# HGRN states, MoBA scores and softmax between the tiles of the projections, HGRN outputs made token by token

## The reference, cut to what matters

```python
hq, hf, hi, hg, mq, mk, mv = jnp.split(h @ w_in, IN_SPLITS, axis=-1)
# HGRN2, per head, chunks of C = 32 tokens
f = lb + (1 - lb) * sigmoid(hf);  k = 1 - f;  b = cumsum(log(f)) within a chunk
q_t = q * exp(b);  k_t = k * exp(-b);  k_end = k * exp(b_last - b)
A = where(causal, q_t @ k_t.T, 0)
o_n = A @ v + q_t @ state            # per chunk n
state = exp(b_last) * state + k_end.T @ v
o = o * rsqrt(mean(o * o, over the 128 of a head) + EPS) * norm_g * silu(hg)
# MoBA: rotary on 32 of 128 features of mq and mk, then
p = softmax(where(causal, mq @ mk.T / sqrt(128), -inf));  o_moba = p @ mv
x = x + concatenate([o_hgrn, o_moba]) @ w_out
```

## Time and profile before

| | before |
|---|---|
| median of 3 runs (lowest, highest) | 862.06 us (860.3, 863.2) |
| the profiled execution: time, span of the core | 863.93 us, 862.1 us |
| granted TensorE clock, mean over the span | 0.963 |
| PE busy | 815.8 us (95%) |
| DVE busy | 565.1 us (66%) |
| ACT busy | 391.2 us (45%) |
| POOL busy | 71.5 us (8%) |
| mean transfer rate over the span | 148 GB/s |

### The profile page before, as it was taken

The page is one execution under the profiler, slowest core; times in us unless marked ns, Lnnn a source line. Parts: engine busy times, 40 slices in busy tenths (PEclk is TensorE's granted clock), DMA queues, the critical chain, the costliest instruction groups (busy, mean ns, idle before and its releaser), DMA issues.

```text
span 862.1 us, 17113 instructions
## 1 busy us (share of the span) xinstructions
PE 815.8 (95%) x7466; PEld 688.3 (80%) x7466; DVE 565.1 (66%) x881; ACT 391.2 (45%) x613; POOL 71.5 (8%) x98
## 2 busy tenths in 40 slices
PE   4999978988999999999999999999998999999996
PEld 3798866777767788888886868597886888888885
DVE  2769975645166889999856777567457566674443
ACT  3546351120053376666754764116256356653333
POOL 1123011202000211111000100000200200000000
PEclk9999996998799999999999999979999999999999
DMA  9772230203004745555586256100482516555201
GB/s 329 290 294 98 98 110 2 101 2 102 1 1 156 272 158 196 195 196 197 195 299 240 98 210 227 52 2 0 177 313 99 194 67 227 196 196 209 86 2 49
DMA packets 66491, 127.93 MB, mean 148 GB/s; under 512 B 3696, under 2 KB 27504, under 8 KB 66288
## 3 DMA queue, kind: packets, MB, share of 16 engines
q1 hardware_dynamic: 65104, 122.92, 39.6%
q0 software_dynamic: 592, 2.69, 0.9%
q10 hardware_dynamic: 720, 1.23, 0.4%
HBM read 125.78 MB, written 1.05 MB: 147 GB/s over the span
## 4 chain that ended last, share of the span: by engine, by line
PE 74%; DVE 15%; ACT 6%; issue 2%; DMA 2%; POOL 0%; DVEq 0%; SPq 0%; ACTq 0%
PE bank L493 21%; PE bank L601 18%; DVE arena L481 7%; PE bank L598 6%; PE bank L699 6%; DVE arena L1865 3%; PE bank L1162 3%; PE bank L1953 3%; DMA ring<-in_w_in_dram 2%; ACT arena L472 2%; PE bank L1414 1%; PE bank L1181 1%; PE bank L2335 1%; PE bank L2077 1%; PE bank L2092 1%
## 5 line engine op out<-in xcount | busy, mean ns | idle before, releaser
L481 DVE SCALAR_TENSOR_TENSOR arena<-ring,arena 128x1024 f16<-128x1024 f32 x194 | 229.5, 1230 | 75.7 <-ACT arena L472 75.3
L493 PE MATMUL bank<-hg,arena 128*128 128x256 f16 x2496 | 275.1, 273 | 1.0 <-DVE arena L481 1.0
L493 PEld LDWEIGHTS bank<-hg,arena 128*128 128x128 f16 x2496 | 243.2, 98 | 32.4 <-issue 2.5
L472 ACT ACTIVATE arena<-ring 128x1024 f16<-128x1024 f32 x194 | 191.9, 1045 | 83.5 <-PE bank L601 51.8
L601 PE MATMUL bank<-arena 128*128 128x256 f16 x1296 | 142.2, 273 | 0.2 <-DVE arena L481 0.2
L601 PEld LDWEIGHTS bank<-arena 128*128 128x128 f16 x1296 | 126.6, 98 | 15.5 <-issue 0.9
L598 PE MATMUL bank<-mix,ring 128*128 128x256 f32 x256 | 55.7, 379 | 1.1 <-ACT arena L1797 1.1
L699 PE MATMUL bank<-hg,ring 128*128 128x256 f32 x224 | 51.5, 391 | 4.7 <-DMA ring<-in_w_in_dram 4.7
L598 PEld LDWEIGHTS bank<-mix,ring 128*128 128x128 f32 x256 | 48.5, 190 | 8.4 <-issue 1.9
L699 PEld LDWEIGHTS bank<-hg,ring 128*128 128x128 f32 x224 | 43.7, 197 | 11.4 <-DMA ring<-in_w_in_dram 5.1
L508 ACT ACTIVATE hg<-h,params 128x256 f16<-128x256 f32 (+1 forms) x48 | 23.9, 499 | 56.4 <-DVE h L2281 42.8
(11 more groups left out here) (365 smaller groups left out, 964.7 us busy)
## 6 DMA issues: line engine op xcount, KB each, us to landing
ring<-in_w_in_dram SPq DMA_DIRECT2D x13, 2048.0 KB, 8.7
ring<-in_ffn_w_up_dram SPq DMA_DIRECT2D x22, 1024.0 KB, 7.4
ring<-in_w_ff_dram SPq DMA_DIRECT2D x8, 2048.0 KB, 9.0
ring<-in_w_ff_dram SPq DMA_DIRECT2D x16, 1024.0 KB, 6.0
ring<-in_ffn_w_down_dram SPq DMA_DIRECT2D x11, 1024.0 KB, 6.3
ring<-in_w_out_dram SPq DMA_DIRECT2D x8, 1024.0 KB, 6.3
ring<-in_w_xk_dram SPq DMA_DIRECT2D x2, 2048.0 KB, 12.0
ring<-in_w_xv_dram SPq DMA_DIRECT2D x2, 2048.0 KB, 8.3
```

What stands on the lines that cost most here:

```text
L472: nc.scalar.activation(quarter(halves_of(chunk)[0], chunk, q), quarter(slot(*chunk), chunk, q), ACT.Copy, scale=W_SCALE).then_inc(*mark("w ...
L481: nc.vector.scalar_tensor_tensor(quarter(halves_of(chunk)[1], chunk, q), quarter(slot(*chunk), chunk, q), W_SCALE, quarter(halves_of(chunk ...
L493: mm = nc.tensor.matmul(out_, weight[a][:, k, cols], src[:, k, b, :], start=(first and i == 0), stop=(last and i == 2), skip_group_check=True)
```

## The change

The order of the mixer on every engine is written anew, some buffers move, and the HGRN outputs change their layout.

- PE: the order is now hi, gate, mq, `pe_hgrn`, then the four tiles of mk with a state behind each and the rotary of mq behind the second, then mv in four pieces of four k-tiles by 512 columns, with states 4 to 6, the rotary of mk, the first output block and the scores of heads 0 and 1 between them, then the second output block, the scores of heads 2 and 3 and the turn of the HGRN outputs.
- HGRN outputs are token-major: for each 128 tokens one bank holds four heads. q~ is the loaded operand, 32 columns at a time, its result at partitions 0, 32, 64 or 96 (`tile_position=(0, r)`), and the state is streamed. The mean of squares is now over a row: ACT squares, DVE sums, ACT takes the root of 128x8, DVE inverts and scales, PE turns the eight tiles back, DVE multiplies by norm and gate.
- w_out_2 takes k-tiles 0 to 3 first; the MoBA transposes stand behind its second k-tile, the MoBA outputs behind its fourth. All four of its banks wait for the last HGRN tile.
- DVE and ACT follow suit; DVE's division of the MoBA probabilities comes behind the HGRN outputs. The scores move to other arena columns and banks (`MOBA_BANK`), and the seven states lie in seven pieces.

```diff
-    out += [("w_out_2", "rows", i) for i in (1, 0)]
+    out += [("w_out_2", "rows", i) for i in range(2)]
...
                             for m in range(KT):
-                            mm = product(i, kk, m)
+                            last_row = product(i, kk, m)
+                    if between and i == 0 and kk % 2:
+                        between(kk // 2)
...
-            feature_major(5, 2, "mk bank", [("hgate scaled", 0), ("hgate scaled", 1)])
             pe_hgrn(pe)
-            pe_rotary(pe)
-            token_major(6, 0, "mv bank", [("mq scaled", 0), ("mq scaled", 1)])
+            for tile in range(4):
+                feature_tile(5, 2, "mk bank", [("hgate scaled", 0), ("hgate scaled", 1)], tile)
+                pe_hgrn_state(pe, tile)
+                if tile == 1:
+                    pe_rotary(pe, 0)
+            pe.wait_ge(*at("low", SPLIT_NO[W2(6)], 3))
+            pe.wait_ge(*at("rotary bank read", 0, 0))
+            token_part(6, 0, 0, "mv bank", range(0, 4))
+            pe_hgrn_state(pe, 4)
+            pe_rotary(pe, 1)
+            token_part(6, 0, 0, "mv bank", range(4, KT))
+            pe_hgrn_state(pe, 5)
+            pe_hgrn_out(pe, 0)
+            pe.wait_ge(*at("rotary bank read", 0, 1))
+            token_part(6, 1, 1, "mv bank", range(0, 4))
+            pe_hgrn_state(pe, 6)
+            pe_moba_scores(pe, (0, 1))
+            token_part(6, 1, 1, "mv bank", range(4, KT))
+            split_used(W2(6), ("mv bank", 1))
+            pe_hgrn_out(pe, 1)
+            pe_moba_scores(pe, (2, 3))
+            pe_hgrn_turn(pe)
...
             scaled(MQ, 0, lambda b: ("mq bank", b), "mq scaled")
+            dve_hgrn(dve)
             split_low(dve, N2 + 6, range(4))
+            for n in (0, 1):
+                dve_hgrn_state(dve, n)
+            dve_rotary(dve, 0)
+            dve_hgrn_state(dve, 2)
             scaled(MK, 2, lambda b: ("mk bank", b), "mk scaled")
+            for n in (3, 4):
+                dve_hgrn_state(dve, n)
+            dve_rotary(dve, 1)
+            for n in (5, 6):
+                dve_hgrn_state(dve, n)
...
+        def pe_hgrn_out(pe, c):
+
+            pe.wait_ge(*at("A", c))
+            pe.wait_ge(*at("k end token-major", c))
+            for j in range(4):
+                nc.tensor.matmul(quarters(6 + c)[:, j, :], AM[c][:, j, :], VI[:, c, j * C:(j + 1) * C],
+                                 start=(j == 0), stop=False, skip_group_check=True)
+            pe.wait_ge(*at("hgrn state", 4 * c + 2))
+            for j in range(4):
+                for n in range(max(1, 4 * c), 4 * c + 4):
+                    r = HG_CHUNK * (n % 4)
+                    mm = nc.tensor.matmul(quarters(6 + c)[r:r + HG_CHUNK, j, :],
+                                          HQ[:, j, n * HG_CHUNK:(n + 1) * HG_CHUNK],
+                                          SV[n - 1][:, j * C:(j + 1) * C], start=False, stop=True,
+                                          tile_position=(0, r), skip_group_check=True)
+            mm.then_inc(*mark("hgrn_pe", "o bank", c))
+
+        def pe_hgrn_turn(pe):
+
+            for c in range(NC_):
+                pe.wait_ge(*at("o unit", c))
+                pe.wait_ge(*at("hgrn state", NS - 2))
                 for j in range(4):
...
+                    mm = nc.tensor.transpose(halves(4 + j // 2)[:, j % 2, c * C:(c + 1) * C],
+                                             ON[:, c, j * C:(j + 1) * C], ident)
+            mm.then_inc(*mark("hgrn_pe", "o turned"))
...
+        def dve_hgrn_unit(dve):
+            dve.wait_ge(*at("o root"))
+            nc.vector.reciprocal(o_rate, o_rate).then_inc(*mark("hgrn_vector"))
+            dve.wait_ge(*so_far("hgrn_vector"))
+            for c in range(NC_):
+                nc.vector.tensor_tensor(ON[:, c, :].rearrange("p (j d) -> p j d", j=4), quarters(6 + c),
+                                        along(o_rate[:, 4 * c:4 * c + 4], C), ALU.mult).then_inc(
+                    *mark("hgrn_vector", "o unit", c))
+
+        def dve_hgrn_end(dve):
+            dve.wait_ge(*at("o turned"))
+            dve.wait_ge(*at("hgate"))
+            for j in range(4):
+                nc.vector.scalar_tensor_tensor(mix[:, j, :], halves(4 + j // 2)[:, j % 2, :], par("hgrn_norm_2", j),
+                                               GH[:, j, :], ALU.mult, ALU.mult).then_inc(
+                    *mark("hgrn_vector", "mix2", j))
...
+            narrow(pe, "w_out_2", KT, mix, lambda k: ("mix2", k), "out2", lambda b: ("mix2", 3),
+                   between=lambda n: (pe_moba_turn, pe_moba_out)[n](pe))
...
+            act_hgrn_squares(act, 0)
+            act_moba_values(act, 0)
+            act_hgrn_squares(act, 1)
+            act_moba_values(act, 1)
+            act_hgrn_root(act)
+            act_moba(act, (0, 1))
+            act_moba(act, (2, 3))
             act_moba_out(act)
...
+            dve_hgrn_sums(dve, 0)
+            dve_moba_masked(dve, (0, 1))
+            dve_hgrn_sums(dve, 1)
+            dve_moba_masked(dve, (2, 3))
+            dve_hgrn_unit(dve)
             dve_hgrn_end(dve)
+            dve_moba_normal(dve)
```

More of the change, by code:

```diff
@@ L1945, in pe_project2, with token_part @@
                         ("post_ffn", "added", 7))
-            def token_major(i, b0, label, waits):
-                pe.wait_ge(*at("low", SPLIT_NO[W2(i)], 3))
+            def token_part(i, c, bank, label, ks):
                 w_ = halves_of(W2(i))
[L1949 to L1954, removed]
+                for k in ks:
+                    for n, (a, b) in enumerate(((0, 0), (1, 0), (0, 1))):
+                        mm = nc.tensor.matmul(banks[bank][:, :], hg16[:, k, b, c * C:(c + 1) * C], w_[a][:, k, :],
+                                              start=(k == 0 and n == 0), stop=(k == KT - 1 and n == 2))
+                if ks[-1] == KT - 1:
@@ L2098, in pe_hgrn_norm, with pe_hgrn_state @@
-        def pe_hgrn_norm(pe):
-            for i in range(2):
-                pe.wait_ge(*at("o squares", i))
-                pe.wait_ge(*at("hgrn state", NS - 2))
-                mm = nc.tensor.matmul(banks[4 + i][:, :], ones, flat(BCS)[:, 512 * i:512 * i + 512],
-                                      start=True, stop=True)
-                mm.then_inc(*mark("hgrn_pe", "o total", i))
+        def pe_hgrn_state(pe, n):
+            c, r = n // 4, 32 * (n % 4)
+            pe.wait_ge(*at("k end token-major", c))
+            pe.wait_ge(*(at("A", n) if n < 2 else at("hgrn state", n - 2)))
+            for j in range(4):
+                mm = nc.tensor.matmul(quarters(4 + n % 2)[:, j, :], KETOK[r:r + 32, c, j * C:(j + 1) * C],
+                                      VI[r:r + 32, c, j * C:(j + 1) * C], start=True, stop=True,
+                                      tile_position=(r, 0))
+            mm.then_inc(*mark("hgrn_pe", "hgrn state bank", n))
@@ L2173, in act_moba_values, with act_hgrn_squares, act_hgrn_root @@
-        def act_moba_values(act):
-            for c in range(NC_):
+        o_rate = lb[:, 16:24]
+        def act_hgrn_squares(act, c):
+            act.wait_ge(*at("o bank", c))
+            nc.scalar.activation(sqs[:, c, :], banks[6 + c][:, :], ACT.Square).then_inc(
+                *mark("hgrn_act", "o squares", c))
+        def act_hgrn_root(act):
+            act.wait_ge(*at("o sums", 1))
+            nc.scalar.activation(o_rate, o_rate, ACT.Sqrt, bias=eps[:, 0:1], scale=1.0 / C).then_inc(
+                *mark("hgrn_act", "o root"))
@@ L2267, in act_moba_out @@
                 act.wait_ge(*at("moba turned", j))
[L2268 removed]
+                nc.scalar.activation(PT[:, j, :], banks[MOBA_BANK[j]][:, 0:3 * C], ACT.Copy).then_inc(
                     *mark("moba_act", "moba p", j))
```

196 lines of the change are left out of this document (74 added, 122 removed).

## The result

The changed kernel takes 853.35 us (median of 8 runs, 852.18 to 857.31), the kernel before 860.24 us in runs beside it (8, 852.99 to 863.2). The ratio is 0.9929, interval 0.9902 to 0.9956; a second, longer comparison gave 0.994, 0.991 to 0.997. The forecast was 852.8 us.

A forecast was written before the change was run, and what follows sets the result against it. It took PE's own instruction list, with thin blocks, their waits and half clock, as the bound. Savings of 18.7 us less costs of 9.4 gave 9.3 saved, from 862.06 to 852.8 us; range 848.5 to 859.5.

The forecast's parts named there:

- seven states: HGRN states on PE: 56 instructions at 0.10 us, 5.6 instead of 9.9, saving 4.3 us.
- product with the states: Token-major HGRN outputs on four column positions overlap: 1.8 us instead of 7.32, saving 5.5; bounds 1.5 and 6.1.
- second output block to w_out: Scores, masks, maxima, root, scalings, transposes and gated outputs up to w_out's start: 7.95 us.
- excursions: About ten switches of PE from full-width projection to a small block and back: 0.15 each, 1.5 us; bounds 1.0, 3.5.
- the wait ahead of w_out: PE idle until the last HGRN tile is ready: costs 5.9 us, bounds 4.5 and 7.5.
- covers: Shifted DVE and ACT work, such as state 0, weight splits and xq splits, stays hidden behind PE: costs nothing.
- rival 1: Clock falls within the interleaved mk and mv stretch too: three falls at 1.7, 5.1 us, 858.0 us; chance 0.19.
- The clock term: After the pause w_out starts at half clock or falls to it: costs 2.0 us.
- Rivals 3 to 5: Better, 849.4 us, 0.11; gain handed back at xq, 857.9, 0.04; half clock for most interleaved work, 872.8, 0.05.
- rival 2: Tiled HGRN outputs don't overlap (4.3 us) and every excursion costs more (1.0): 858.1 us; chance 0.11.

The follow-up runs named there:

- experiment 8: Changed kernel with HGRN states in pairs, mq's rotary behind mk's third tile: stretch 83.0 us against 85.8; with the second output block also earlier 76.5, ratio 0.986.
- experiment 4: Changed kernel with each of the two rotary blocks cut in two: stretch from A products to xq 83.7 us in both traces, against 85.8.
- experiment 6: Changed kernel with second output block a quarter of mv earlier, ACT and DVE steps reordered: stretch 79.9 us against 85.8; ratio to kernel before 0.9856, again 0.9887.

## Why the prediction was right, and where it was not

The time, 852.8 against 853.35, and the direction came out. The saving did not: 9.3 us were forecast, the stretch shows 4.7 and the ratios 5 to 6. That the time hit nevertheless is luck in two parts: the three runs shown of before lie 1.8 us above the median of the eight, and the medians differ by 2.2 us more than the stretch does, for which the forecast has no term.

| term | forecast | measured |
|---|---|---|
| A, turn of k | 2.65 | 2.66 |
| four tiles of mk | 10.48 | 12.53 |
| mv | 10.4 | 10.66 |
| rotary | 3.68 | 3.67 |
| seven states | 5.6 | 7.59 |
| first two scores | 1.32 | 1.42 |
| A times V | 1.78 | 2.07 |
| product with the states | 1.8 | 2.02 |
| second output block to w_out | 7.95 | 9.30 |
| w_out, MoBA, half clock behind the wait | 33.8 | 33.88 |
| excursions, as a term of their own | 1.5 | in the rows above |
| sum | 81.0 | 85.8 |

- **Right:** the cause (thin work in one block, its waits and its half clock), the tiled product (2.02 for 1.8, where the bounds reached to 6.1), the scores and transposes at full clock, the wait ahead of w_out and the half clock behind it (2.3 for 2.0), all covers: state 0, the weight splits and xq were nowhere late, xq followed w_out at once.
- **Mis-sized: the excursions.** States 2.0 more than at 0.10 each, tiles of mk 0.4, mv 0.3, A times V 0.3, scores 0.1: 3.0 instead of 1.5, within the bound of 3.5. The larger part is a row misread: the 0.10 per instruction was taken from eleven instructions of two neighbouring states in the kernel before, and these ran partly side by side (their starts, 557.44 to 558.87, have the same pattern as the pair of experiment 8). A lone state has no neighbour: eight at 0.112 are 0.9, its two ends take 0.2, and the tile before takes 0.1 more.
- **Left to a rival: the fall in mk.** 1.65 us, rival 1 with one of its three falls, at the place it named. The block there had been counted as 2.6 us of thin work; it was 2.9 (experiment 4).
- **Mis-sized: the chain.** 9.30 instead of 7.95. The turn ran at half clock, 0.9 more (1.97 us for the eight, 1.04 at full clock in experiment 6), and w_out began 0.4 behind DVE's last output (570.90 and 1.66, to 572.92), which was counted as nothing. The clock term had only w_out in it, not the transposes ahead. (The forecast's wait, 5.9, should by its own terms have been 7.95 less 2.15, 5.8.)
- **Not seen: that much of this wait was of the order's making.** I summed the chain as written and didn't ask what DVE did in it that w_out didn't need: masks and maxima of heads 2 and 3, from 564.99 to 567.92, 2.9 us in a chain of 9.3, and ACT's copy of mv ahead of its root. Experiment 6 shortened the chain by 2.4, filled another 1.3 with mv and took out the half clock at w_out.

Rivals 3 to 5 didn't come, and of rival 2 only the second half: no output block took 0.1 us per instruction, but the excursions cost 1.5 more, where it had 1.0. The wait stayed above its lower bound, no time was handed back at xq, and the interleaved stretch ran at full clock but for 3.4 us. The Trainium skill's figure for three column positions ("TensorE: Matmul & The Clock Gate", Part 3), 2.38 times, would give an estimated 2.6 for the tiled product; measured were 2.02, so in this case the overlap was better: 6.1 over 2.02 is 3.0 times, and the block with three positions alone (24 x 0.109 over 1.01) 2.6 times. The Trainium skill's "TensorEngine Tiling (Array Packing)", Key Properties, has a change of mode drain the array; the 0.3 us that a lone state pays at its ends and on the tile before agrees that it costs, without showing a drain.

## What to carry to other kernels

Thin products between full tiles hide the elementwise work between them, and here mostly kept the clock: it held in all six traces with visits of at most 2 us there, and fell in five of six at one of 2.9, though never at a second one of 2.9, nor at the 3.2 us of a state, A times V and the tiled products. A visit has a price, here 0.3 us; more was gained by putting two together that lie on different rows of the array, since they run partly side by side. For the same reason an average over a block of such products is no price for one that will stand alone: look at the distances between single starts. Where PE has to wait for a chain on other engines, go through that chain for steps that the waiting instruction doesn't need, and put them behind it; in three of four traces here the half clock after the wait went with them. And compare kernels by the stretch that the edit touches, where another stage scatters by more than the edit is worth.

## What the runs showed of the hardware

- Products of 128 rows by 32 columns, 128 columns streamed, float32: 0.032 to 0.042 us per instruction at four and three column positions in turn, 0.075 to 0.08 when four products (eight instructions) in a row had the same position. PE overlapped neighbouring groups by itself, and started instructions of the later group ahead of the last ones of the earlier.
- Eight instructions of 32x128: 1.09 us alone between other shapes, 1.64 for sixteen on two different row groups, the second of which started 0.55 us behind the first, beside its last four.
- Falls of the clock lasted 3.4 us (in mk), 6.8 or 10.2 us (behind the wait: 567.2 to 577.5 in the changed kernel). A fall of 3.4 us over full tiles cost 1.65.
- The RWKV stage, the same instructions in all kernels, ended anywhere within 10 us. Its mean granted clock from 140 to 240 us lay between 0.83 and 0.91, low in the late ones and high in the early ones (0.86 at 245.5, 0.85 at 247.3). What makes the clock fall more in one execution than in another was not tried and stays open. Behind w_out_2 the rest took 243.0 to 243.7 us in twelve traces and 241.5 in two.
